# Broadcasting cumulative decays by DMA in place of segment-sum matmuls, in a hybrid SSD, sparse-attention and PEER layer

## What is computed

```python
def segsum(a):
    cs = jnp.cumsum(a, -1)
    diff = cs[..., :, None] - cs[..., None, :]
    return jnp.where(jnp.tril(jnp.ones((T, T), dtype=bool)), diff, -jnp.inf)
# in ssd_chunked, for each chunk of 128 tokens and each head
a_cs = jnp.cumsum(a, -1)
Lmat = jnp.exp(segsum(a))                                 # [l, s] for each head
CB = jnp.einsum('bclgn,bcsgn->bgcls', Cc, Bc)
scores = CB[:, :, None] * Lmat
y_diag = jnp.einsum('bgkcls,bcsgkp->bclgkp', scores, xdt)
```

## Time and profile before

| | |
|---|---|
| median of 3 runs | 945.32 us (944.87 to 945.9) |
| the profiled execution, its own time | 946.71 us |
| its span, first to last instruction | 944.9 us |
| TensorE busy / VectorE / ScalarE / GpSimd | 80% / 63% / 46% / 31% of the span |
| mean granted TensorE clock | 0.831 of full speed |
| moved by DMA | 337.43 MB, 268.45 MB of it by GpSimd's queue |

### The profile page before, as it was taken

How to read it: one execution, slowest core, us unless ns; L and a number is a source line. 1 busy time by engine, 2 the same in 40 slices (tenths; PEclk the granted TensorE clock), 3 DMA queues, 4 the chain that set the end, 5 groups by cost and what they waited for, 6 DMA issues and landing times.

```text
span 944.9 us, 11753 instructions
## 1 busy us (share of the span) xinstructions
PE 758.0 (80%) x4042; PEld 346.3 (37%) x4044; DVE 593.5 (63%) x1423; ACT 430.9 (46%) x1182; POOL 291.1 (31%) x295
## 2 busy tenths in 40 slices
PE   8999999999879999889685866767767766666674
PEld 6886665655634434433121522232311111011110
DVE  1625241647598978685666665787667766767445
ACT  1144205632479988664334433363443434434333
POOL 0010012001254434343242333334433344344330
PEclk9999999999978989989695867787965666677766
DMA  7633255737999999999999999999999999999993
GB/s 270 255 121 123 69 233 189 300 126 288 426 417 405 414 422 420 421 421 422 423 424 419 423 419 421 421 420 422 420 421 421 422 420 422 421 420 422 420 421 120
DMA packets 45788, 337.43 MB, mean 357 GB/s; under 512 B 6048, under 2 KB 6048, under 8 KB 9120
## 3 DMA queue, kind: packets, MB, share of 16 engines
q0 software_dynamic: 37152, 268.45, 68.6%
q1 hardware_dynamic: 8576, 68.22, 18.2%
HBM read 335.61 MB, written 1.05 MB: 356 GB/s over the span
## 4 chain that ended last, share of the span: by engine, by line
DMA 42%; PE 38%; ACT 8%; DVE 6%; issue 4%; POOL 2%; DVEq 0%; SPq 0%; POOLq 0%; ACTq 0%
DMA late<-in_uv,eidx 17%; DMA ring<-in_uv,eidx 14%; DMA wring<-in_uv,eidx 11%; PE ps L1120 7%; PE ps L709 6%; PE ps L733 6%; PE ps L860 5%; ACT late L1169 4%; ACT L1169 3%; PE ps L903 3%; PE ps L716 1%; PE ps L725 1%; DVE ring L1910 1%; DVE late L1910 1%; ACT tmp L1169 1%
## 5 line engine op out<-in xcount | busy, mean ns | idle before, releaser
L1169 ACT ACTIVATE late<-late 128x1 f32<-128x1 f32 (+3 forms) x787 | 222.4, 285 | 331.5 <-DVE late L1910 307.7
L1120 PE MATMUL ps<-ring,late 64*64 64x512 f32 x928 | 168.8, 817 | 83.0 <-ACT late L1169 76.9
L1120 PE MATMUL ps<-late 64*64 64x512 f32 x960 | 162.3, 770 | 72.8 <-ACT late L1169 65.5
L1910 DVE CUSTOM_DVE_ANT_0 late<-late,x_sb 128x1024 f32<-128x1024 f32 x120 | 146.9, 1225 | 86.2 <-DMA late<-in_uv,eidx 81.4
L2009 POOL DMA_INDIRECT late<-in_uv,eidx x118 | 126.2, 1069 | 234.7 <-PE ps L1120 174.1
L1910 DVE CUSTOM_DVE_ANT_0 ring<-ring,x_sb 128x1024 f32<-128x1024 f32 x116 | 142.1, 1225 | 85.8 <-DMA ring<-in_uv,eidx 80.6
L2009 POOL DMA_INDIRECT ring<-in_uv,eidx x116 | 125.2, 1080 | 198.1 <-PE ps L1120 187.3
L1169 ACT ACT_TABLE_LOAD x85 | 109.1, 1283 | 27.3 <-PE ps L725 14.6
L1120 PEld LDWEIGHTS ps<-ring,late 64*64 64x64 f32 x928 | 30.5, 162 | 186.7 <-ACT late L1169 161.6
L1120 PEld LDWEIGHTS ps<-late 64*64 64x64 f32 x960 | 31.7, 157 | 177.7 <-ACT late L1169 146.0
L1169 ACT ACTIVATE tmp<-ps 128x512 f32<-128x512 f32 (+4 forms) x87 | 43.6, 508 | 67.3 <-PE ps L709 41.2
(11 more groups left out here) (265 smaller groups left out, 770.1 us busy)
## 6 DMA issues: line engine op xcount, KB each, us to landing
wring<-in_wts SPq DMA_DIRECT2D x21, 2048.0 KB, 9.9
ring<-in_wts SPq DMA_DIRECT2D x2, 2048.0 KB, 10.7
wring<-in_wts SPq DMA_DIRECT2D x2, 1428.0 KB, 5.8
wring<-in_wts SPq DMA_DIRECT2D x2, 1388.0 KB, 7.1
lnw<-in_ln SPq DMA_DIRECT2D x4, 512.0 KB, 12.5
late<-in_uv,eidx POOLq DMA_INDIRECT x118
ring<-in_uv,eidx POOLq DMA_INDIRECT x116
wring<-in_wts SPq DMA_DIRECT2D x3, 512.0 KB, 6.9
```

The costliest lines, as they stand in the source:

```text
L1120: last = mm(o[t][n * HD:(n + 1) * HD, :], factor[tokens, :], values[tokens, n * 512:(n + 1) * 512], start=start, stop=stop, skip_group_che ...
L1169: return nc.scalar.activation(out, in_, func, **kw)
L1910: V.tensor_tensor_reduce(out=u_row, in0=u_row, in1=h_sb[:, i, :], scale=1.0, scalar=0.0, op0=ALU.mult, op1=ALU.add, accum_out=hdot[:, e, k ...
```

## The change

The segment sum is no longer a matmul. Two more small matmuls in decay_sums put the cumulative sums with heads on 16 partitions. ScalarE copies them to SBUF (`sums_T`) and SP writes them to a DRAM buffer `decay_sums` of 2 x 8 KB, waits for that, and reads each 8 KB row back to all 128 partitions, 1 MB a chunk, into `ring3`. VectorE then takes for each quarter a minimum with, and a subtraction of, the sum of the row's own token. ScalarE's exponentials read SBUF. The four 512-column products of each chunk, `Ma` and its eight bank turns are gone.

Around it, TensorE's tm 3 moves ahead of chunk_sums(0), and tm 4 ahead of chunk_sums(1). ScalarE's copy of tm 2 moves ahead of the exponentials of chunk 0, and its copy of tm 3 to just behind them. The exponentials of chunk 1 wait until TensorE has finished the products of chunk 0. SP's load of the second gate's weights waits for the last exponential.

```diff
@@ TensorE's order
     chunk_scores(0)
     tokens("tm", 2, widths[2])
+    tokens("tm", 3, widths[3])
     chunk_sums(0)
     chunk_scores(1)
-    tokens("tm", 3, widths[3])
+    tokens("tm", 4, widths[4])
     chunk_sums(1)
-    tokens("tm", 4, widths[4])
     tokens("tm", 5, widths[5])
@@ SP
+                if k == 8:
+                    sp.wait_ge(sums_ready, 1)
+                    for i in range(NT):
+                        sp.dma_start(sums_out[i:i + 1, :].rearrange("i (h l) -> (i h) l", h=NH), sums_T[:, i, :]).then_inc(sums_written, 16)
+                    sp.wait_ge(sums_written, 16 * NT)
+                    for i in range(NT):
+                        sp.dma_start(decay[i].rearrange("p h l -> p (h l)"), sums_out[i:i + 1, :].to_broadcast([P, NH * P])).then_inc(decay_here[i], 16)
                 if k == 10:
-                    await_full(sp, "seg", 1, 3)
+                    sp.wait_ge(E_ready, 8)
                     sp.dma_start(ring3[:, :], wts[:, starts[11]:starts[12]]).then_inc(wz_here, 16)
@@ decay_sums and chunk_scores, TensorE
+                    last = mm(o[0:NH, 256 + i * P:256 + (i + 1) * P], a_sb[:, i, :], tri, start=True, stop=True)
                 filled(last, "acs")
...
                 filled(last, "cb", i)
-                pe.wait_ge(Ma_ready, i + 1)
-                for n in range(4):
-                    o = await_free(pe, "seg", i, n)
-                    filled(mm(o, strict, Ma[:, 4 * n:4 * n + 4, :].rearrange("p h l -> p (h l)"), start=True, stop=True), "seg", i, n)
@@ ScalarE
             def decays(i):
+                if i:
+                    await_full(act, "yd", 0, NG - 1)
                 for n in range(4):
-                    o = await_full(act, "seg", i, n)
-                    taken(f(E[:, 4 * n:4 * n + 4, :], o.rearrange("p (h l) -> p h l", h=4), ACT.Exp), "seg", i, n)
+                    act.wait_ge(decay_ready, 4 * i + n + 1)
+                    f(E[:, 4 * n:4 * n + 4, :], decay[i][:, 4 * n:4 * n + 4, :], ACT.Exp).then_inc(E_ready, 1)
...
             o = await_full(act, "acs")
+            f(sums_T, o[0:NH, 256:256 + NT * P].rearrange("h (i l) -> h i l", i=NT), ACT.Copy).then_inc(sums_ready, 1)
+            f(sums, o[:, 0:NT * 2 * NH].rearrange("p (i n h) -> p i n h", i=NT, n=2)[:, :, 0, :], ACT.Copy)
             taken(f(ea[:, :, :, :], ...
+            token_rows(2)
             decays(0)
-            token_rows(2)
+            token_rows(3)
@@ VectorE
-            def chunk_masks(i):
-                dve.wait_ge(a_ready, 1)
-                tt(Ma, bc(tri, 1, NH), bc(a_sb[:, i, :], 2, P), ALU.mult).then_inc(Ma_ready, 1)
+            def chunk_differences(i):
+                dve.wait_ge(decay_here[i], 16)
+                await_taken(dve, "acs")
+                for n in range(4):
+                    d = decay[i][:, 4 * n:4 * n + 4, :]
+                    s = bc(sums[:, i, 4 * n:4 * n + 4], 2, P)
+                    link(tt(d, d, s, ALU.min))
+                    tt(d, d, s, ALU.subtract).then_inc(decay_ready, 1)
...
-            chunk_masks(0)
             for i in range(NT):
                 chunk_weights(i)
+                if i == 0:
+                    chunk_differences(0)
                 chunk_decays(i)
                 if i == 0:
-                    chunk_masks(1)
+                    chunk_differences(1)
                 chunk_outputs(i)
```

## The result

| | before | changed |
|---|---|---|
| median | 945.9 us (944.87 to 946.41, 5 runs) | 939.69 us (937.9 to 941.29, 5 runs) |
| ratio of the runs | | 0.9931, 95% interval 0.9919 to 0.9942 |
| profiled execution: its own time / span | 946.71 / 944.9 us | 939.81 / 937.9 us |
| TensorE, VectorE, GpSimd busy | 758.0, 593.5, 291.1 us | 757.0, 599.6, 299.6 us |

The kernel became 6.2 us faster by the medians, 5.5 to 7.7 by the interval. The forecast was 6.4.

What follows compares the result with a forecast made beforehand. TensorE was taken to bound the kernel before 256 us, the DMA engines after. 6.88 - 0.45 = 6.43 us off TensorE, nothing lost elsewhere, gave 940.3 profiled and a 938.9 us median; range 937.0 to 943.2.

Steps and rivals of the forecast that it cites:

- The bound: Whole kernel: TensorE bounds it before 256 us, the DMA engines after; a microsecond off TensorE ends it a microsecond earlier.
- Part 1: TensorE's SSD products: 6.88 us of segment products go, two small matmuls add 0.45, net 6.43 us off.
- Part 2: Route of the sums through DRAM to the scores: decays land at 94.5, first quarter ready at 100.6, no TensorE stall.
- The room: Ahead of chunk_sums(0): the first quarter of scores is ready 3.7 us before TensorE wants it at 104.3.
- Part 3: Work behind the new waits on SP, VectorE and ScalarE: all of it costs 0; VectorE's ropes end about 137.
- A: Ahead of chunk_sums(0): decays land at 100 to 103, stall 1.8 to 4.8 us, 940.7 to 943.7 us; chance 0.11.
- D: After 134 us: something that does not move with TensorE absorbs the gain, 945.3 us; chance 0.07.
- B: Broadcasts from one 8 KB row are slow; at 12.5 us each, 949 us; chance 0.05 together with C.
- C: TensorE's clock halves in a 3 us stall, tm 4 at half clock, 951 us; chance 0.05 together with B.
- B's two limits: Cost for a broadcast of B us: first stalls TensorE beyond 6.8; from about 7.9, piece 8 queued behind, 2B - 14.9.

Runs made afterwards that it cites:

- e5: Changed kernel with four 512-column products of constants put back into each chunk_scores, ahead of the CB products; 946.98 us, ratio 1.0005 to the kernel before.
- e2: Changed kernel with SP writing the sums to DRAM three more times, each after the last completed, before the broadcasts; 941.62 us, ratio 0.9959 to the kernel before.
- e3: Changed kernel with SP writing the sums to DRAM six more times in series before the broadcasts; 952.18 us, ratio 1.0064 to the kernel before.
- e1: Changed kernel with SP writing the sums to DRAM one more time in series before the broadcasts; 939.99 us, ratio 0.9939 to the kernel before.
- e4: Changed kernel with tm 3, tm 4 and ScalarE's copy of tm 3 back in their old places, new decays kept; 950.67 us, ratio 1.0047 to the kernel before.
- e9: Changed kernel with SP writing the sums to DRAM four more times in series before the broadcasts; 948.04 us, ratio 1.0019 to the kernel before.
- e8: Changed kernel with SP writing the sums to DRAM five more times in series before the broadcasts; 950.53 us, ratio 1.0039 to the kernel before.
- e6: Kernel before, segment products kept, with only the changed kernel's token piece order and ScalarE's copy of tm 3 moved; 946.22 us, ratio 0.9994.
- e10: e4 plus six 512-column products of constants on TensorE just ahead of its wait for the scores; 945.63 us, ratio 0.9993 to the kernel before.

## Why the prediction was right, point by point

- **The bound.** TensorE before 256 us, the DMA engines after. Right: e5 gives 7.1 us of TensorE for 7.3 us of time, and the last stretch is equally long in both kernels within 0.4 us (690.3 and 689.9).
- **Part 1, TensorE's work.** 6.88 us gone, as said. The two new products were taken at 0.45 and took 0.32 + 0.32 = 0.64, outside the 0.54 that I had set as the bound. I had priced them by the row of CB, and that row itself goes from 0.44 to 0.64 in the changed kernel with what stands ahead of it. That term was 0.2 too small, and the old four products and CB became 0.1 longer each: from the start of decay_sums to the end of tm 5 it is 134.85 - 83.43 = 51.42 us for 141.02 - 83.58 = 57.44, so 6.0 us less, where the sum has 6.43. The span of the profiled execution shrank by 7.0. Of the other 1.0, 0.15 was there before decay_sums began, 0.45 came between tm 5 and the first rows added, and 0.4 behind it. Executions of one kernel differ by more (937.9 to 941.3), so this 1.0 is not put down to the change.
- **Part 2, the route.** The copy of the sums took 0.37 us for 0.4, the sums were in DRAM at 89.8 for 89.7, the decays landed at 94.67 for 94.5, the differences took 5.4 us for 5.4, and the first quarter was ready at 100.7 for 100.6. The room was 3.9 us for 3.7. What made this come out is that the queue ahead of the write was counted: the 16 KB wait for piece 7's last bytes, so that the first write takes 89.80 - 85.41 = 4.4 us where a later one takes 1.80 (e2, e3). One term was too large: with 0.9 us to the first data, e1's expectation made a round trip 2.2 us, 0.4 too long. The estimate with the 2.0 us of the Trainium skill ("DMA: Bandwidth & Descriptors", section "Anatomy of one DMA"), 96.9, was too late by 2.2 us, and would have changed nothing; the page gives that figure for transfers that GpSimd issues, and these are SP's.
- **Part 3, what waits behind.** Piece 8 was issued at 94.97, the load for the second gate at 112.60 (113 expected, 116.89 before), and no wait of TensorE came with them. VectorE's tail moved to 135.32 + 1.63 = 136.95 (137 expected). The number is right by luck. The two ropes took 7.6 us before (124.68 to 132.26), so that an end at 137 has them start at 129.4. They started 1.3 us earlier, at 128.13, and the second took 1.2 us longer, beside GpSimd. VectorE's next product came at 151.07, with 150.8 expected.
- **The rivals.** A and D did not happen. B had no ground, at 397 GB/s. C's mechanism is real: e4, e9, e8 and e3 all show it. It sits between 5.0 us (e2, room and wait together) and 7.1 us (e9) of lateness away. I priced a stall of 3 us at 12.6 us, with tm 4 at half clock. e9's wait of 3.2 us cost 8.4, for it was the short products of chunk_sums(0) that ran at half speed, and the clock was back 0.7 us before tm 4, which took its usual 9.62 us. In rival A, I had a late landing cost one for one over 1.8 to 4.8 us of stall. By e9 and e8, a stall of 3.2 to 4.9 us costs 8 to 11 and ends slower than the kernel before. So A's place in the prediction was wrong: from some length between 1.1 and 3.2 us of stall on, A is C. Two details of the rivals don't hold either. B's two limits, B - 6.8 and 2B - 14.9, meet at 8.1 and not at 7.9. And the 579 ns that C reads from the earlier trace rows for the stretch 605:610 belong to another time: the trace has no L903 product there. What half clock costs is shown by chunk_sums(0) instead, 3.52 us at 1.00 and 7.06 at 0.50.
- **The numbers.** 938.9 for 939.69 measured. Of the 0.8 between them, 0.6 is the kernel before, whose median came out at 945.9 beside the changed kernel and not at 945.3; the gain itself was 6.2 for 6.4. The profiled execution was 940.3 for 939.81, where 0.4 too much on TensorE and the 1.0 from elsewhere partly cancel.

## What to carry to other kernels

Where one engine is busy from end to end, take work from it and give it to whichever engine or queue is idle, however many steps the new way has, but lay the steps out against the time at which the result is wanted, counting what is queued ahead of each transfer. Then move independent work of the busy engine into that gap, as the changed kernel does with tm 3 and tm 4: the order was worth nothing by itself (e6), the new decays without it lost 4.6 us against the kernel before as measured beside them (e4), and the two together won 6.2. For TensorE a gap of some length (here 3.2 us and more, not 1.1) is dearer than itself, so that even dead products in it can pay (e10).

## What the runs showed of the hardware that I had not expected

- A wait of TensorE of 1.1 us left its clock at 1.00; waits of 3.2, 4.9, 5.5 and 6.5 us took it to 0.50. It stayed there for 10.2 to 11.6 us of SSD products, though the engine was busy without a break, and the return is not tied to the next token piece: in e9 and e3 it came before that piece began.
- A write of 2 x 8 KB to DRAM and its completion, seen from SP, takes 1.80 us from issue to issue, 0.8 of it the two issues.
- VectorE and GpSimd products on SBUF can slow each other, by a third on VectorE (4.88 for 3.65 us) and up to threefold on GpSimd (1.43 for 0.46), though one VectorE product beside GpSimd kept its 1.23 us.
